# Twelve gate products between an attention, a recurrence and their merge: a two-layer hybrid backbone on one core

## What is computed

```python
hl = modulate(rmsnorm(xl, norm1_g[l]), sh1, sc1)            # sh, sc, g: silu(c) @ w_ada[l] + b_ada[l]
z  = split_cols(hl @ w_in[l])
da = diff_attention(...)      # softmax(q1 k1) - lam * softmax(q2 k2), 4 heads
ml = mlstm_mixer(...)         # a chunked recurrence, forwards and backwards
cv = short_conv(...)
g_da, g_ml, g_cv = jnp.split(sigmoid(gate), 3, axis=-1)     # gate = the last 3072 columns of hl @ w_in
m  = g_da * (y_da @ w_da) + g_ml * (y_ml @ w_ml) + g_cv * (y_cv @ w_cv)
xl = xl + g1 * (m @ w_o)
xl = xl + g2 * peer(modulate(rmsnorm(xl, norm2_g[l]), sh2, sc2), ...)   # product keys, 128 experts a token, gathered
```

## Time and profile before

| what | us |
|---|---|
| median of 3 executions (5317.77 to 5326.93) | 5321.41 |
| the profiled execution, its own time | 5306.48 |
| its span, first to last instruction | 5304.4 |
| TensorE matmul busy | 3960.9 (75%) |
| VectorE busy | 2773.6 (52%) |
| ScalarE busy | 1727.5 (33%) |
| GpSimd (gathers) busy | 1473.8 (28%) |
| mean granted TensorE clock | 0.865 |

### The profile page before, as it was taken

One profiled execution on the slowest core, in us unless ns is written; L12 is line 12 of the kernel. 1 busy time (PEld: TensorE's weight loads), 2 busy tenths in 40 slices (PEclk: granted clock), 3 DMA queues, 4 the chain that ended last, 5 costly groups with the idle time before them and its releaser, 6 DMA issues.

```text
span 5304.4 us, 62645 instructions
## 1 busy us (share of the span) xinstructions
PE 3960.9 (75%) x21784; PEld 2365.2 (45%) x21784; DVE 2773.6 (52%) x6649; ACT 1727.5 (33%) x4737; POOL 1473.8 (28%) x1295
## 2 busy tenths in 40 slices
PE   5998697989986886677576677897667997655554
PEld 4676564656753553333233234676234664211111
DVE  1313757565358446765455443434676447844444
ACT  1210247342433543333222222221335353322222
POOL 0000022232223333333343441000332233345453
PEclk8899899899997998888787888799788998777677
DMA  6346477678998999999999995225996999899998
GB/s 252 142 159 247 156 287 279 262 288 301 374 371 328 369 420 391 394 394 386 384 420 399 404 421 229 83 86 207 381 376 253 355 391 392 322 416 421 401 421 352
DMA packets 265341, 1712.60 MB, mean 323 GB/s; under 512 B 37600, under 2 KB 39232, under 8 KB 77632
## 3 DMA queue, kind: packets, MB, share of 16 engines
q0 software_dynamic: 184320, 1342.26, 63.2%
q1 hardware_dynamic: 80704, 366.33, 18.6%
HBM read 1690.46 MB, written 17.92 MB: 322 GB/s over the span
## 4 chain that ended last, share of the span: by engine, by line
PE 43%; DMA 23%; DVE 16%; ACT 6%; issue 4%; POOL 3%; DVEq 2%; ACTq 2%; PEld 1%; SPq 0%; PEldq 0%; another core or an unknown queue 0%; POOLq 0%
PE psum L504 28%; DMA arena<-in_uv,arena 20%; PE psum L894 10%; DVE arena L2268 6%; POOL arena L1263 3%; DVE arena L2171 1%; DVE arena L2164 1%; DVE arena L2165 1%; PE psum L449 1%; ACT arena L1360 1%; DMA arena<-in_w_ada 1%; PEld psum L504 1%; DMA arena<-in_norm_g 1%; DVE arena L2237 1%; DVE arena L2239 1%
## 5 line engine op out<-in xcount | busy, mean ns | idle before, releaser
L1263 POOL DMA_INDIRECT arena<-in_uv,arena x1280 | 1469.9, 1148 | 3796.1 <-PE psum L894 2549.4
L894 PE MATMUL psum<-arena 64*64 64x512 f32 x10240 | 1533.0, 727 | 907.7 <-ACTq L1651 826.3
L2268 DVE CUSTOM_DVE_ANT_0 arena<-arena 128x1024 f32<-128x1024 f32 x1280 | 1547.8, 1225 | 1118.9 <-DMA arena<-in_uv,arena 1055.2
L504 PE MATMUL psum<-arena 128*128 128x256 f32 (+2 forms) x8480 | 1966.4, 390 | 142.8 <-DVEq L1670 100.3
L504 PEld LDWEIGHTS psum<-arena 128*128 128x128 f32 (+1 forms) x8480 | 1620.6, 195 | 589.4 <-issue 184.6
L894 PEld LDWEIGHTS psum<-arena 64*64 64x64 f32 x10240 | 383.5, 154 | 1826.4 <-ACTq L1651 1155.6
L1644 ACT ACTIVATE arena<-arena 128x2 f32<-128x2 f32 x640 | 130.8, 204 | 1534.7 <-DVEq L2270 1498.6
L1650 ACT ACTIVATE arena<-arena 128x64 f32<-128x64 f32 x1280 | 375.8, 340 | 45.0 <-issue 0.7
L1647 ACT ACTIVATE arena<-arena 128x1 f32<-128x1 f32 x1280 | 307.6, 287 | 46.8 <-issue 3.0
L449 PE MATMUL psum<-arena 128*128 128x128 f32 (+1 forms) x680 | 114.7, 318 | 166.8 <-DVE arena L1731 46.2
L1644 ACT ACT_TABLE_LOAD x158 | 202.7, 1283 | 30.8 <-DVEq L2270 27.3
(11 more groups left out here) (203 smaller groups left out, 2394.3 us busy)
## 6 DMA issues: line engine op xcount, KB each, us to landing
arena<-in_w_in SPq DMA_DIRECT2D x92, 1024.0 KB
arena<-in_w_mix SPq DMA_DIRECT2D x88, 768.0 KB
arena<-in_w_ada SPq DMA_DIRECT2D x32, 1536.0 KB, 11.0
arena<-in_w_wq SPq DMA_DIRECT2D x40, 1152.0 KB
arena<-in_w_mix SPq DMA_DIRECT2D x24, 1024.0 KB
arena<-in_w_wo SPq DMA_DIRECT2D x20, 1024.0 KB
arena<-in_uv,arena POOLq DMA_INDIRECT x1280
arena<-ada_rows SPq DMA_DIRECT2D x15, 512.0 KB, 4.4
```

What stands on the lines that cost most here:

```text
L504: ins = mm(out, a, b, start=(i == 0), stop=(i == last))
L894: ins = mm(psum[o, r_ * 512:r_ * 512 + 512], DIAG[rows, c, :], RING[rows, sl, D + half * 512:D + (half + 1) * 512], start=first, stop=last ...
L1263: pool.indirect_dma_start(RING[:, sl, :], None, io["uv"], bass.IndirectOffsetOnAxis(IDX[:, t, h * TOPK + k:h * TOPK + k + 1], 0)).then_inc ...
L2268: V_.tensor_tensor_reduce(out=RING[:, sl, 0:D], in0=RING[:, sl, 0:D], in1=XT[:, u % 2, :], scale=1.0, scalar=0.0, op0=ALU.mult, op1=ALU.ad ...
```

## The change

Two things are changed. First, a table `GATE_DA` takes some gate chunks out of the recurrence and puts them into the attention in front of it, each behind the product with V of a given unit: chunks 0 and 2 behind units 1 and 3 of `da` in layer 0 on the context, and chunks 8, 9, 10, 11 behind units 0, 2, 4, 6 of `da` in layer 1 on pair 1. ScalarE's Sigmoid for them stands behind the exponentials of the next unit. The chunks left over are numbered through: in layer 0 the four units of `ml` get (1, 3), (4, 5), (6, 7), (8, 9), the first early and the second late, and `mln` keeps 10 and 11. In layer 1 the six units of `ml_back` get one early chunk each, 0 to 5, and none late, and `mln` gets 6 and 7. `chunk_list` and SyncE's `chunks` follow. Second, TensorE's part of `ada(2)` stands ahead of the second half of V in `qkv` instead of behind the stage's last step, that of `ada(4)` ahead of the second half of `mlv` in `mlp`, and that of `ada(5)` ahead of the last `bg` step in `mc`. VectorE's part of the three stays where it was.

```diff
--- before.py
+++ after.py
@@ -76,17 +76,27 @@
 GATE_CHUNKS, GATE_TAIL = 3 * KD // 2, 2
 
 
+GATE_DA = {(0, (0,)): {1: 0, 3: 2}, (1, (1,)): {0: 8, 2: 9, 4: 10, 6: 11}}
+
+
+def scan_chunks(kind, l, pairs):
+    p = AHEAD[kind, l, pairs]
+    rest = [n for n in range(GATE_CHUNKS) if n not in GATE_DA[l, (p,)].values()]
+    return rest[:len(rest) - GATE_TAIL]
+
+
 def gate_chunks(kind, l, pairs, i, late):
-
     if (kind, l, pairs) not in AHEAD:
-        return range(0)
-    per = GATE_CHUNKS // len(ml_units(kind, l, pairs))
-    all_ = range(per * i + 1, per * i + per) if late else range(per * i, per * i + 1)
-    return [n for n in all_ if n < GATE_CHUNKS - GATE_TAIL]
+        return []
+    mine, n = scan_chunks(kind, l, pairs), len(ml_units(kind, l, pairs))
+    mine = mine[len(mine) * i // n:len(mine) * (i + 1) // n]
+    return mine[1:] if late else mine[:1]
 
 
 def tail_chunks(l, pairs):
-    return range(GATE_CHUNKS - GATE_TAIL, GATE_CHUNKS) if (l, pairs[0]) in AHEAD_OF else range(0)
+    if (l, pairs[0]) not in AHEAD_OF:
+        return []
+    return [n for n in range(GATE_CHUNKS) if n not in GATE_DA[l, pairs].values()][-GATE_TAIL:]
 
 
 DEFERRED = ((0, (0,)), (1, (1,)), (1, (2,)))
@@ -221,7 +231,9 @@
             elif kind == "edge":
                 out += [(l, "in", CHUNK_NAMES.index((name, hh))) for hh, name in EDGE_OPS]
             elif (kind, l, pairs) in AHEAD:
-                out += [(l, "gate", i) for i in range(GATE_CHUNKS - GATE_TAIL)]
+                out += [(l, "gate", i) for i in scan_chunks(kind, l, pairs)]
+            elif kind == "da" and (l, pairs) in GATE_DA:
+                out += [(l, "gate", i) for i in GATE_DA[l, pairs].values()]
             elif kind == "mln":
                 out += [(l, "gate", i) for i in tail_chunks(l, pairs)]
             elif kind == "merge":
@@ -542,6 +554,8 @@
 
             def qkv(kind, l, pairs):
                 for op in qkv_ops(kind):
+                    if (l, pairs) == FIRST and op == ("v", 1):
+                        ada(2)
                     if op[0] != "turn":
                         w = view(weights(l, "in", CHUNK_NAMES.index(op)), [KD, PW])
                     for p in pairs:
@@ -561,8 +575,6 @@
                         if op[0] != "turn" and p == pairs[-1]:
                             weights_done()
                         yield
-                if (l, pairs) == FIRST:
-                    ada(2)
                 barrier()
 
             def heads_turned(l, p, which, src):
@@ -606,6 +618,8 @@
                     for kt in range(nk):
                         ins = mm(psum[:, 3840:3840 + P], wt[:, kt * P:(kt + 1) * P], V[:, kt, h * P:(h + 1) * P], start=(kt == 0), stop=(kt == nk - 1))
                     ins.then_inc(s("da_o"), 1)
+                    if (l, pairs) in GATE_DA and u in GATE_DA[l, pairs]:
+                        gates_ahead(l, pairs[0], [GATE_DA[l, pairs][u]])
                     if (l, pairs) == FIRST and u == 5:
                         ada(3)
                     yield
@@ -637,6 +651,8 @@
                             weights_done()
                         yield
                 for c in range(2):
+                    if (l, pairs) == FIRST and c:
+                        ada(4)
                     w = view(weights(l, "in", CHUNK_NAMES.index(("mlv", c))), [KD, PW])
                     for p in pairs:
                         ht = buf(l, p, "HT", [KD, PW])
@@ -664,7 +680,6 @@
                 yield
                 if (l, pairs) == FIRST:
                     heads_turned(0, 0, "day", buf(0, 0, "YD", [2, W5]))
-                    ada(4)
                 barrier()
 
             def ml(kind, l, pairs):
@@ -754,6 +769,8 @@
                             if (l, pairs) in DEFERRED:
                                 heads_turned(l, p, "day", buf(l, p, "YD", [2, W5]))
                             heads_turned(l, p, "mly", ym_of(l, p, (l, p) == (1, 2)))
+                    if (l, pairs) == FIRST and (hh, name) == (1, "bg"):
+                        ada(5)
                     w = view(weights(l, "in", CHUNK_NAMES.index((name, hh))), [KD, PW])
                     for p in pairs:
                         ht = buf(l, p, "HT", [KD, PW])
@@ -763,8 +780,6 @@
                         if p == pairs[-1]:
                             weights_done()
                         yield
-                if (l, pairs) == FIRST:
-                    ada(5)
                 barrier()
 
             def edge(kind, l, pairs):
@@ -1030,7 +1045,9 @@
                     ada_load(3)
                 nrow = buf(l, pairs[0], "NRD", [P])
                 sp.dma_start(nrow, io["da_subln_g"][l:l + 1, :].to_broadcast([P, P])).then_inc(s("nrow"), 16)
-                for u in da_units(l, pairs):
+                for u, unit in enumerate(da_units(l, pairs)):
+                    if (l, pairs) in GATE_DA and u in GATE_DA[l, pairs]:
+                        chunks(1)
                     yield
                 barrier()
                 if (l, pairs) in DEFERRED:
@@ -1369,6 +1386,8 @@
                     A.activation(wt[:, 0:nk * P], psum[:, 3072:3072 + nk * P], ACT.Copy).then_inc(s("da_wt"), 1)
                     if u + 1 < len(units):
                         exps(u + 1)
+                    if (l, pairs) in GATE_DA and u in GATE_DA[l, pairs]:
+                        gates_sigmoid(l, pairs[0], [GATE_DA[l, pairs][u]])
                     yield
                 barrier()
                 if (l, pairs) in DEFERRED:
```

## The result

| | before | after |
|---|---|---|
| median, us (6 executions each) | 5324.84 | 5338.21 |
| lowest to highest | 5317.77 to 5326.93 | 5330.35 to 5345.94 |
| ratio, 95% interval | | 1.0027 [1.0015, 1.0039] |
| the profiled execution, own time | 5306.48 | 5344.94 |
| its span | 5304.4 | 5343.1 |

What follows compares the result with a forecast made beforehand. TensorE was taken to bound the recurrences, while the attentions looked as if they had idle time. Layer 0's -6.9 and layer 1's +9.6 gave +3 us: 5309.5 for the profiled execution, 5324 for the median, range 5309 to 5338.

Steps and rivals of the forecast that it cites:

- the clock term of the backward recurrence: `ml_back`, layer 1: clock falls in most thinned units cost +6 us, a better-clocked start returns -3, within -16.6 in all.
- Rival 2: The clock falls in the thinned backward recurrence, 4.0 us in each of four units: +16 us, 5337; chance 0.2.
- The attention of layer 1: `da` of layer 1: four gate products inside its loop lengthen the stage by 26.2 us, bounds +19 and +34.
- Rival 1: The attentions' idle TensorE time can be filled, so both cost 10 us instead of 41: -28, 5293; chance 0.13.
- the table question: ScalarE's table reloads in the attentions: 1.3 us each by the trace; the skill's 1.38 drain would add 6.9 over five.
- The attention of layer 0: `da` of layer 0: two products cost 16.9 us, full clock behind them returns 1.7 and `ada(3)` 0.7: +14.5.
- The recurrence of layer 0: `ml`: three late products leave, -21.0; last unit +2.4, bank wait +3.3, clock +1: -14.3 us, and -2.8 behind it.
- The quarters: Moved `ada` parts in layer 0: `qkv` -1.8, end of `mlp` -3.1, end of `mc` +0.6, together -4.3 us.
- Rival 3: The products keep the clock up in both attentions and `ml_back`: -12 us from the forecast, 5312; chance 0.12.
- rival 4: A moved `ada` quarter waits for its weights behind gate chunks in the queue: up to some 10 us, 5334; chance 0.07.

Runs made afterwards that it cites:

- Filler: The changed kernel with four unread matmuls added behind the turned keys in units 0 to 3 of `ml_back`: 5323.3 us, 1.0008 of the kernel before.
- banks: The changed kernel with layer 0's attention chunks reordered so no unit of `ml` has two products in one bank: 5331.18 us, 1.0017 of the kernel before.
- repaired: The changed kernel with layer 0's chunks reordered against bank conflicts and four unread matmuls in `ml_back`'s units 0 to 3: 5320.6 us, 0.9994 of before.
- quarters: The kernel before with only TensorE's part of the three conditioning quarters, `ada(2)`, `ada(4)` and `ada(5)`, moved: 5321.24 us, ratio 1.0003.
- spread: The kernel before with one late product moved from unit 2 to the last unit of layer 0's recurrence `ml`: 5314.39 us, ratio 0.9983.

## Why the prediction was wrong

**The step that failed is the clock term of the backward recurrence**, "I take such a fall in most of the units: +6", with "With a product in the tail I expect half of it back: -3". Forecast was -19.6 + 6 - 3 = -16.6, measured -8.6. *Filler* splits it: without the falls the stage changes by -22.3, so -19.6 for the products (the unit of 16.88 bears it out) and -3 for its start were right within 0.3. The falls cost 13.7, not 6. I had priced one from a pause of 2.4 us behind which the level stayed low for 3.5 us; here two waits, 1.25 and 1.99, with 0.7 us of work between them came with 6.8 to 10.2 us of it, over half of the blocks and the start of the product, 3.4 a unit in each of the four. Rival 2 described just that, at 4.0 a unit. Of the two parts that it adds to the forecast, the falls (+10) came with +7.7, and the lost gain at the start (+3) was not lost. That its 5337 lies so near the measured 5338 is luck to that extent: layer 0 added what these two didn't. The rival had 0.2 of the chances, and its threshold of "two full falls a unit" misplaced where it decides: one fall in each unit was enough. The Trainium skill (TensorE: Matmul & The Clock Gate, A second HAM failure mode: psum-queue depth-cycling) says that short idle times between groups of matmuls make the clock oscillate. This trace agrees (four falls at four pairs of 1.25 and 1.99), and by that page the rival deserved more than I gave it.

**The attention of layer 1** (+26.2, measured +25.5) was right: 7.9 for unit 0 and 7.1 each for units 2 and 4, where 7.9 and 7.3 were forecast, and 3.4 behind unit 6, where 4.7 - 1.0 was. How long the half level at its start lasts moves the sum, +23.4 in *filler* and *banks*; *repaired*, whose start has before's levels, gives +25.2. With it the reading that idle time in a loop of three engines isn't free was right. Rival 1 is out. Both sides of the table question are measured: 1.28 of load, the exponential 1.30 behind the load's start, and a whole switch costs 0.8 on the path. The drain of 1.38 us for every switch that the Trainium skill gives (ScalarE: Activation LUTs, What ACT_TABLE_LOAD costs) isn't seen in this case. By it the three units would have been some 6.5 longer in all than with a copy, an estimate from that page and the 0.8; the measured difference was 2.4.

**The attention of layer 0** (+14.5, measured +17.3): "In return the units behind it run at full level" failed. The two units right behind a product did, 0.65 shorter each, but the level fell again between the products, and the second one began at half level (8.96, not 7.0). The unit with `ada(3)` took 0.8 more and the end 0.8 more, each under another fall, so the expected return of 1.7 + 0.7 came to nothing.

**The recurrence of layer 0** (-14.3, measured -11.2): the bank's wait is 3.30 against 3.3; what I took as "+1 for the clock behind that pause" was 2.5, as the product behind it took 9.81 instead of 7.10 and *banks* gives 5.8 for the two. The rest, 1.6, I put down to the half level at the stage's start: of the stretch of 24 us, 19.7 lie in this stage, where before had 17.1. Behind it, `mc` does start at full level (-1.8, forecast -2.8 + 0.6). `mln` (-1.7, forecast 0) was left out of the sum: the half level from 397.5 to 401.0 at its start, from which I had my price of a fall, is not there in the changed kernel:

```profile
397.50:401.00 3.50, 3.41 (x16) 3.00 (x17) 0.00 (x0) 0.00 (x0) 0.00 (x0) 1.00 0.37 94
```

**The quarters** (-4.3; +1.7 by themselves): `qkv` gave its 1.8; its end lies at 118.2 on average over the five kernels with the quarter in its old place (117.7 to 119.2) and at 116.5 over the eight others (115.8 to 118.0). For `mlp` I forecast an end 57.6 behind the stage's start; in *banks* it is 57.5, but in the changed kernel 59.25. There the clock fell 4 us ahead of the barrier, and the small matmuls on the way to it took 2.62 and 1.97, where they take 1.92 and 1.09 in *banks*:

```profile
227.42 2.62 PE L678 MATMUL psum<-arena 36*128 36x2 f32 x16
...
229.97 1.97 PE L461 MATMUL psum<-arena 128*128 128x128 f32 x8
```

```profile
227.88 1.92 PE L678 MATMUL psum<-arena 36*128 36x2 f32 x16
...
229.73 1.09 PE L461 MATMUL psum<-arena 128*128 128x128 f32 x8
```

Both kernels execute the same instructions there, and ahead of them the same shapes in the same order, with other chunks of weights. What differs is when the level changed: in the attention ahead it was first at half level from 3.2 to 13.4 us into the stage in the changed kernel, and from 4.7 to 15.0 in *banks*. Where exactly a level falls moved by a few us from kernel to kernel, and each quarter that ended a stage earlier met another phase behind it. I had treated what a stage gains as the kernel's, "what they gain or lose", and that holds for the barriers but not for the clock across them. That *quarters* gives 1.5 back in `da` under other levels is seen in its trace; what set those levels is not shown by an experiment of its own. Rival 3 is out, rival 4 too: none of the three moved quarters waited for its weights.

The sum: +3 forecast, +15.1 in the trace. 8.0 of the 12.1 lie in `ml_back`, 2.8 and 3.1 in layer 0's attention and recurrence; the rest (`mlp` +1.7, `mln` -1.7, `merge` -1.3 and smaller ones) nearly cancels.

## What to carry to other kernels

A product taken out of a loop that TensorE bounds saves less than its length when it leaves pauses: first count the wait that comes back, then what the clock does behind it, and price the second for every turn of the loop. Idle time in a latency-bound loop takes work only in pieces smaller than its gaps: one piece of 7.0 cost 7.1, eight of 0.9 cost nothing. The place that paid here was the pause at a stage's end: the product that *spread* put there cost its own stage 2.3 in place of 7.0, and the stage behind it, now started at full level, was 2.6 shorter. And a gain of 1 or 2 us in one stage of one trace says little when the clock's level differs: look at the level in both traces first, and compare stages that ran under the same.

## What was unexpected of the hardware

Four unread matmuls a unit, in four units, each 1.9 us of work that nobody uses, made a stage 13.7 us (11.5%) shorter. The clock's level also depends on more than a stage's own work: identical sequences of instructions ran at 0.73 of the full clock in one kernel and at 1.00 in another, in the last 7.6 and 7.7 us of the same stage. These are their two windows, with the same columns:

```profile
core 0: us, PE busy (x) PEld busy (x) DVE busy (x) ACT busy (x) POOL busy (x), PEclk, DMA share, GB/s
225.00:232.60 7.60, 6.20 (x38) 5.32 (x36) 0.00 (x0) 5.26 (x7) 0.00 (x0) 0.73 0.00 0
```

```profile
224.00:231.70 7.70, 6.08 (x45) 5.18 (x43) 0.00 (x0) 4.92 (x7) 0.00 (x0) 1.00 0.00 0
```
